# A gated recurrence's decay factors: the 64-token level and the decays to a chunk's end computed by ScalarE with a bias per row

## The chip, the cores and the metric

One core of one Trainium2 chip runs the kernel. The metric is the device time of one execution in microseconds (us). Its engines work in parallel, each through its own queue in order: PE (TensorE, the matmuls; PEld is its weight load), DVE (VectorE), ACT (ScalarE), POOL (GpSimd), and SP (SyncE), which here only issues DMAs.

## The reference, cut to what matters

The whole is one decoder layer with three parallel token mixers (a gated linear recurrence "A", a gated recurrence "B" with a convolution, and sparse attention "C"), for a prompt of 1024 tokens and 8 samples of one token each. Only mixer A on the prompt matters here, four heads of 128 keys by 128 values:

```python
    log_f = jnp.logaddexp(jnp.log(lb), jnp.log1p(-lb) + jax.nn.log_sigmoid(af.astype(jnp.float32)))
    ka = -jnp.expm1(log_f)
    ...
    def step(S, xs):
        qi, ki, vi, gi = xs
        b = jnp.cumsum(gi, axis=2)
        inter = jnp.einsum('bhtk,bhkv->bhtv', qi * jnp.exp(b), S)
        diff = b[:, :, :, None, :] - b[:, :, None, :, :]
        decay = jnp.exp(jnp.where(causal, diff, -jnp.inf))
        att = jnp.sum(qi[:, :, :, None, :] * ki[:, :, None, :, :] * decay, axis=-1)
        intra = jnp.einsum('bhts,bhsv->bhtv', att, vi)
        b_last = b[:, :, -1:, :]
        S_new = jnp.exp(b_last[:, :, 0, :])[..., None] * S + jnp.einsum('bhsk,bhsv->bhkv', ki * jnp.exp(b_last - b), vi)
```

## The kernel before, in words

PE makes all projections as three matmuls for each product (a high and a low part of both operands), and this fills most of the time. In the part about mixer A the projections of head h (the items P0 to P11; for the last pass G0 to G11, the merge gates' projections) are interleaved by hand with the recurrence of head h-1. Every engine walks the same written list, `a_items(h)` (lines 578 to 595), for five passes h = 0 to 4. The items that matter:

- P0 to P11: projections. P3 to P5 give the forget gate. At P5 ScalarE makes two passes over the whole row (Exp, then Ln, lines 1894 and 1895), then VectorE four (lines 2397, 2398, the scan 2400 and 2401), which give `b`, the running sum of the log decay, and `bk`, which is `b` minus the key's logarithm. The event `a_scan` follows.
- F (once per head) and R0, R2, R4 (one each): a *batch* of factors for 256 tokens (two chunks of 128), four batches for each head, 16 in all. GpSimd makes differences of `b` and `bk` into a ring `DD` of 6 slots (`differences`), ScalarE takes Exp of each into the tile `XQ` (`a_exps`), VectorE multiplies the query half of each by `q` (`a_factors`, lines 2417 and 2411).
- R0 to R7: one chunk of 128 tokens each. PE multiplies the factors of all levels (`a_levels`, line 1492 for the levels 64, 32 and 16), VectorE masks and adds them (lines 2427, 2428, 2431), PE turns the decayed keys (line 1504, copied back by ScalarE at line 1944) and, one chunk later, multiplies with the values and the state (`a_output`, lines 1517 to 1520). PE may start the levels of a chunk only when VectorE has masked the chunk before (`att_masked`, fired by line 2428) and when the batch is done (`x_ready`).
- Q, then N two items later in the next pass: ScalarE squares a head's output (line 1949); PE sums it with ones (lines 1535 and 1538), ScalarE takes Ln and Exp (lines 1960 and 1962).
- S: the samples' states on GpSimd (line 969 and on). GpSimd also splits each weight half into its high and low part (lines 907 and 908) at fixed items.

The chunk of 128 tokens is divided in levels 64, 32, ... 1: in each block of 2m tokens the keys of the first half get exp(b[middle] - bk), the queries of the second exp(b - b[middle]). With the two that are left, the decay of the keys to the chunk's end and exp(b - bk) for the diagonal, a batch has 9 differences. Items of the batch for level m are two GpSimd operations (lines 953 and 954), the other two one each (961 to the chunk's end, 956 for the diagonal). Each operation waits for its own end before the next is issued (`Steps`, line 151). `d_exp` counts a batch's Exps, nine for each.

The order around the third batch of a head (q = 2) is, on PE: P4, R2 (levels of chunk 2, output of chunk 1), P5, R3, P6, (in odd passes P7,) R4. In ScalarE's queue the batch stands in R2, ahead of P5's work; in VectorE's queue the products stand ahead of P5's four passes, and those ahead of R3's mask.

Of the kernel before, what the change touches and what calls it, by code (L numbers as in the profile page):

```python
# [22 lines left out]
ACT = mybir.ActivationFunctionType  # L23
AX = mybir.AxisListType.X
MUL, ADD, SUB, MAX, MIN = ALU.mult, ALU.add, ALU.subtract, ALU.max, ALU.min

P = 128
D = 1024
KT = D // P
NS = 8  # L30
# [241 lines left out]
def layer_program(nc, ctx, a, o):  # L272

    def sb(name, off, shape, dt=F32, parts=P):
        n = 1
        for x in shape:
            n *= x
        size = n * (2 if dt == BF16 else 4)
        assert 4 * off + size <= 4 * END, (name, off, size)
        t = nc.alloc_sbuf_tensor_at(name, [parts] + list(shape), dt, offset=BASE + 4 * off)  # L280
        return t[tuple([slice(None)] * (len(shape) + 1))]
# [163 lines left out]
    XQ = sb("xq", o_, [2, 10, XR]); o_ += 2 * 10 * XR  # L445
    DD = sb("dd", o_, [ND, XR]); o_ += ND * XR
    EL = sb("el", o_, [2, 2]); o_ += 8
    SGA = sb("sga", o_, [TC]); o_ += TC
    MSK = sb("msk", o_, [6, P]); o_ += 768
    STA = sb("sta", o_, [P]); o_ += 128  # L450
# [71 lines left out]
    def e(name):  # L522

        if name not in ev:
            ev[name] = sem(name)
        return ev[name]  # L540
# [336 lines left out]
    def _(pool):  # L877
# [59 lines left out]
        def differences(h, q):  # L937

            S = AS[h % 2]
            c0 = NS + XR * q  # L940
            pool.wait_ge(e("a_scan"), h + 1)
            for i in range(9):
                kk = (4 * h + q) * 9 + i
                if kk >= ND:
                    pool.wait_ge(e("d_exp"), kk - ND + 1)
                dd = DD[:, kk % ND]
                if i < 7:
                    m = LEVELS[i]
                    bv = S["b"][:, c0:c0 + XR].rearrange("p (n two m) -> p n two m", two=2, m=m)
                    dv = dd.rearrange("p (n two m) -> p n two m", two=2, m=m)  # L950
                    ref = bv[:, :, 0, m - 1:m].to_broadcast([P, XR // (2 * m), m])
                    kv_ = S["bk"][:, c0:c0 + XR].rearrange("p (n two m) -> p n two m", two=2, m=m)
                    st(nc.gpsimd.tensor_tensor(dv[:, :, 0, :], ref, kv_[:, :, 0, :], SUB))
                    st.fire(nc.gpsimd.tensor_tensor(dv[:, :, 1, :], bv[:, :, 1, :], ref, SUB), e("d_ready"))
                elif i == 8:
                    st.fire(nc.gpsimd.tensor_tensor(dd, S["b"][:, c0:c0 + XR], S["bk"][:, c0:c0 + XR], SUB), e("d_ready"))
                else:
                    bv = S["b"][:, c0:c0 + XR].rearrange("p (n m) -> p n m", m=P)
                    ref = bv[:, :, P - 1:P].to_broadcast([P, XR // P, P])
                    kv_ = S["bk"][:, c0:c0 + XR].rearrange("p (n m) -> p n m", m=P)  # L960
                    st.fire(nc.gpsimd.tensor_tensor(dd.rearrange("p (n m) -> p n m", m=P), ref, kv_, SUB), e("d_ready"))

        def sample_states(h):

# [689 lines left out]
    def _(act):  # L1654
# [267 lines left out]
        def a_exps(h, q):  # L1922
            S = AS[h % 2]
            c0 = NS + XR * q
            qq = 4 * h + q
            act.wait_ge(e("a_scan"), h + 1)
            if qq >= 2:
                act.wait_ge(e("chunk_full"), 2 * (qq - 1))
            for i in range(9):
                kk = qq * 9 + i  # L1930
                act.wait_ge(e("d_ready"), kk + 1)
                st(A(XQ[:, qq % 2, i if i < 7 else i + 1, :], DD[:, kk % ND], ACT.Exp), e("d_exp"))
            if qq >= 2:
                act.wait_ge(e("s_ready"), 2 * (qq - 1))

            st(A(XQ[:, qq % 2, 7, :], S["b"][:, c0:c0 + XR], ACT.Exp))
            bl = S["b"][:, c0:c0 + XR].rearrange("p (n m) -> p n m", m=P)[:, :, P - 1:P]
            st(A(EL[:, qq % 2, :].rearrange("p (n o) -> p n o", o=1), bl, ACT.Exp), e("eb_ready"))

# [115 lines left out]
    def _(v):  # L2055
# [327 lines left out]
        def a_group(h, i):  # L2383
            S = AS[h % 2]
            c = i % 3
            cc = slice(CH * c, CH * c + CH)
            if i < 3 or (i >= 6 and h % 2):
                n = a_product(h, i)
                v.wait_ge(e("sg_ready"), n + 1)
                if i < 3:  # L2390
                    dst = S["q"][:, cc]
                else:
                    dst = AS[(h - 1 if i < 9 else h) % 2]["z"][:, cc]
                st(stt(dst, in0=SGA[:, cc], scalar=1.0, in1=ps[:, 1 - n % 2, 0:CH], op0=ADD, op1=MUL), pq.free)
            if i == 5:
                v.wait_ge(e("sp_ready"), h + 1)
                st(stt(S["bk"], in0=S["b"], scalar=0.0, in1=SGA, op0=MAX, op1=ADD))
                st(stt(S["b"], in0=S["b"], scalar=0.0, in1=SGA, op0=MIN, op1=SUB), e("a_lf"))

                st(V.tensor_tensor_scan(S["b"][:, NS:TC], RM, S["b"][:, NS:TC], 0.0, MUL, ADD))  # L2400
                st(tt(S["bk"][:, NS:TC], S["bk"][:, NS:TC], S["b"][:, NS:TC], ADD), e("a_scan"))

        def a_factors(h, q):
# [240 lines left out]
```

## Time and profile before

| | us |
|---|---|
| median of 3 runs | 1803.81 |
| lowest and highest | 1794.69, 1806.71 |
| the profiled execution | 1793.93 |
| its span, first to last instruction | 1792.1 |

In the profile a row of the timeline is: start, duration, engine, line, operation, what it writes and reads by the program's names, shapes, how many instructions; in brackets the idle time of the engine ahead of it and what ended it. Times of day are us from the span's start. The recurrence lies at 1045 to 1360.

### The profile page before, as it was taken

The page shows a single profiled execution, that of the slowest core. Times are in us where ns is not written, and L with a number is a line of the kernel's source. Part 1 is how long each engine was busy: PE and PEld are TensorE (multiplying, and loading weights), DVE is VectorE, ACT ScalarE, POOL GpSimd, SP SyncE. Part 2 cuts the span into 40 slices and gives each one's busy share as a digit, 9 for nine tenths or more (in the row PEclk, how much of TensorE's full clock was granted, in tenths as well). Part 3 has the DMA queues.
Part 4 walks back from the last instruction along what each step waited for, and adds up shares of the span by engine and source line. Part 5 has one row for each costly group of instructions (what it writes and reads, how often), then busy time and mean ns, then how long its engine had stood idle before and what let it go on. Part 6 is the DMA issues. An engine that isn't in the chain of part 4 may idle for free. (4 is left out here: it accounts for less than half of the span.)

```text
span 1792.1 us, 30521 instructions
## 1 busy us (share of the span) xinstructions
PE 1612.0 (90%) x11996; PEld 1418.2 (79%) x11996; DVE 901.9 (50%) x1431; ACT 562.7 (31%) x1111; POOL 473.8 (26%) x461
## 2 busy tenths in 40 slices
PE   7899988988896799999989998989899986999997
PEld 3788975666665688888869998888799976899997
DVE  1651366666661222332223358857873373557577
ACT  0312135545451323222211233626352466000100
POOL 2012101000002112111131357657663122135500
PEclk9899999999998899999999999989999998999999
DMA  9321120000004444434223301202032110544422
GB/s 303 125 60 49 25 84 1 1 1 1 1 2 109 111 113 123 115 107 126 75 93 121 119 25 36 68 29 73 25 97 74 26 50 25 171 143 149 167 84 83
DMA packets 162433, 142.89 MB, mean 80 GB/s; under 512 B 50902, under 2 KB 152306, under 8 KB 161522
## 3 DMA queue, kind: packets, MB, share of 16 engines
q1 hardware_dynamic: 153298, 127.20, 23.5%
q10 hardware_dynamic: 8992, 13.74, 2.2%
q8 instruction: 95, 1.56, 0.4%
q14 instruction: 48, 0.39, 0.1%
HBM read 115.62 MB, written 29.40 MB: 81 GB/s over the span
## 5 line engine op out<-in xcount | busy, mean ns | idle before, releaser
L1016 PE MATMUL ps<-w_hi,h_hi 128*128 128x256 f32 x792 | 228.5, 289 | 5.9 <-DVEq L151 2.9
L1016 PE MATMUL ps<-w_lo,h_hi 128*128 128x256 f32 x792 | 223.7, 282 | 0.0
L1016 PE MATMUL ps<-w_hi,h_lo 128*128 128x256 f32 x792 | 223.6, 282 | 0.0
L1016 PE MATMUL ps<-h_hi,w_hi 128*128 128x344 f32 x600 | 199.1, 332 | 3.1 <-ACT ak L1960 1.4
L1016 PE MATMUL ps<-h_lo,w_hi 128*128 128x344 f32 x600 | 193.2, 322 | 0.0
L1016 PE MATMUL ps<-h_hi,w_lo 128*128 128x344 f32 x600 | 192.7, 321 | 0.0
L1016 PE MATMUL ps<-h_hi,wg_hi 128*128 128x344 f32 x432 | 146.3, 339 | 14.2 <-ACT gate_stage L1806 13.3
L1016 PEld LDWEIGHTS ps<-w_hi,h_hi 128*128 128x128 f32 x792 | 150.9, 191 | 8.0 <-DVEq L151 3.3
L1016 PEld LDWEIGHTS ps<-w_hi,h_lo 128*128 128x128 f32 x792 | 150.8, 190 | 0.0
L1016 PEld LDWEIGHTS ps<-w_lo,h_hi 128*128 128x128 f32 x792 | 150.8, 190 | 0.0
L907 POOL CAST w_hi<-w_raw 128x1024 fp32r<-128x1024 f32 (+1 forms) x48 | 52.5, 1094 | 356.2 <-DMA w_raw<-in_w_in 165.9
L1016 PE MATMUL ps<-h_lo,wg_hi 128*128 128x344 f32 x432 | 140.5, 325 | 0.0
L1016 PE MATMUL ps<-h_hi,wg_lo 128*128 128x344 f32 x432 | 140.2, 324 | 0.0
L1016 PEld LDWEIGHTS ps<-h_hi,w_hi 128*128 128x128 f32 x600 | 114.7, 191 | 6.3 <-issue 3.9
L1016 PEld LDWEIGHTS ps<-h_lo,w_hi 128*128 128x128 f32 x600 | 114.3, 191 | 0.7 <-issue 0.2
L1016 PEld LDWEIGHTS ps<-h_hi,w_lo 128*128 128x128 f32 x600 | 114.2, 190 | 0.0
L908 POOL TENSOR_TENSOR w_lo<-w_raw,w_hi 128x1024 fp32r<-128x1024 f32 (+1 forms) x48 | 112.9, 2352 | 3.8
L918 POOL TENSOR_TENSOR qt<-qt,to 128x512 f32<-128x512 f32 x16 | 20.3, 1267 | 331.6 <-DVE to L2242 331.6
L1016 PEld LDWEIGHTS ps<-h_hi,wg_hi 128*128 128x128 f32 x432 | 83.6, 193 | 29.8 <-issue 14.5
L1755 ACT ACTIVATE pr<-ps,nm 128x640 f32<-128x640 f32 (+7 forms) x128 | 88.6, 698 | 54.0 <-DVE nm L2203 42.5
L1225 PE MATMUL ps<-const_g,pr 128*128 128x128 f32 x560 | 82.0, 279 | 21.0 <-ACT pr L1755 8.2
L1806 ACT ACTIVATE gate_stage<-ps 128x344 f32<-128x344 f32 x54 | 24.7, 458 | 214.9 <-PE ps L1016 212.5
(446 smaller groups left out, 3623.4 us busy)
## 6 DMA issues: line engine op xcount, KB each, us to landing
w_raw<-in_w_in SPq DMA_DIRECT2D x46, 512.0 KB, 4.9
sgm<-gate_spill SPq DMA_DIRECT2D x22, 516.0 KB, 6.2
gate_spill<-gate_stage ACTq DMA_DIRECT2D x54, 172.0 KB, 2.4
w_raw<-in_w_in SPq DMA_DIRECT2D x34, 256.0 KB, 4.4
adw<-in_ada_w SPq DMA_DIRECT2D x8, 1024.0 KB, 11.3
pgc<-in_cache_nsa_kv SPq DMA_DIRECT2D x128, 64.0 KB, 2.4
pg<-in_cache_nsa_kv SPq DMA_DIRECT2D x64, 128.0 KB
w_raw<-in_w_branch SPq DMA_DIRECT2D x12, 512.0 KB, 5.2
```

The source lines that it names most:

```text
L907: st(nc.gpsimd.tensor_copy(hi[:, k, 0:width], raw))
L908: st.fire(nc.gpsimd.tensor_tensor(lo[:, k, 0:width], raw, hi[:, k, 0:width].bitcast(F32), SUB), half_split)
L918: st(nc.gpsimd.tensor_tensor(d3, d3, TO[:, i % 2, :].rearrange("p (a c) -> p a c", a=4), ADD), e("to_added"))
L1016: last = mm(out, lhsT=l, rhs=r, start=(first and i == 0 and j == 0), stop=(final and i == n - 1 and j == 2), skip_group_check=joint)
L1225: last = nc.tensor.transpose(ps[:, 4 + way, P * i:P * i + P], PR[:, u % 2, P * j:P * j + P], ID)
L1755: st.fire(A(PR[:, u % 2, P * n * g:P * n * g + P * n], src, ACT.Exp, bias=NM[:, 4 * (u % 2) + g:4 * (u % 2) + g + 1], scale=-1.0, accum_ou ...
L1806: st(A(GST[:, s], ps[:, 1, 0:CH], ACT.Tanh, scale=0.5), gate_free)
```

## The change

The 64-token level and the decays to the chunk's end no longer go through GpSimd. ScalarE's activation computes func(scale * in + bias) with a bias for each partition (each of the 128 keys), and within one chunk these references are one column. For the level 64 that makes four activations of 64 columns (two for each chunk of the batch), for the chunk's end two of 128. The negative of `b` in the chunk's middle, which the query half needs as bias, is made by one VectorE operation per head (128x8) between the scan and the pass of line 2401. GpSimd makes 7 differences a batch in place of 9; the diagonal's is now the seventh. ScalarE does the level 64 first, then the seven from the ring (levels 32 to 1, diagonal), then the two of the chunk's end; the events still count nine for each batch.

```diff
+    NMID = sb("nmid", o_, [2, NT]); o_ += 16
...
             pool.wait_ge(e("a_scan"), h + 1)
-            for i in range(9):
-                kk = (4 * h + q) * 9 + i
+            for kk, i in enumerate((1, 2, 3, 4, 5, 6, 8), 7 * (4 * h + q)):
                 if kk >= ND:
-                    pool.wait_ge(e("d_exp"), kk - ND + 1)
+                    pool.wait_ge(e("d_exp"), 9 * ((kk - ND) // 7) + (kk - ND) % 7 + 2)
                 dd = DD[:, kk % ND]
...
-                elif i == 8:
+                else:
                     st.fire(nc.gpsimd.tensor_tensor(dd, S["b"][:, c0:c0 + XR], S["bk"][:, c0:c0 + XR], SUB), e("d_ready"))
-                else:
-                    bv = S["b"][:, c0:c0 + XR].rearrange("p (n m) -> p n m", m=P)
-                    ref = bv[:, :, P - 1:P].to_broadcast([P, XR // P, P])
-                    kv_ = S["bk"][:, c0:c0 + XR].rearrange("p (n m) -> p n m", m=P)
-                    st.fire(nc.gpsimd.tensor_tensor(dd.rearrange("p (n m) -> p n m", m=P), ref, kv_, SUB), e("d_ready"))
...
-            for i in range(9):
-                kk = qq * 9 + i
+            half = XR // 2
+            for x in range(2):
+                k0 = c0 + half * x
+                st(A(XQ[:, qq % 2, 0, half * x:half * x + 64], S["bk"][:, k0:k0 + 64], ACT.Exp, bias=S["b"][:, k0 + 63:k0 + 64], scale=-1.0))
+                st(A(XQ[:, qq % 2, 0, half * x + 64:half * x + half], S["b"][:, k0 + 64:k0 + half], ACT.Exp, bias=NMID[:, h % 2, 2 * q + x:2 * q + x + 1]),
+                   e("d_exp") if x else None)
+            for kk, i in enumerate((1, 2, 3, 4, 5, 6, 9), 7 * qq):
                 act.wait_ge(e("d_ready"), kk + 1)
-                st(A(XQ[:, qq % 2, i if i < 7 else i + 1, :], DD[:, kk % ND], ACT.Exp), e("d_exp"))
+                st(A(XQ[:, qq % 2, i, :], DD[:, kk % ND], ACT.Exp), e("d_exp"))
+            for x in range(2):
+                k0 = c0 + half * x
+                st(A(XQ[:, qq % 2, 8, half * x:half * x + half], S["bk"][:, k0:k0 + half], ACT.Exp, bias=S["b"][:, k0 + half - 1:k0 + half], scale=-1.0),
+                   e("d_exp") if x else None)
...
                 st(V.tensor_tensor_scan(S["b"][:, NS:TC], RM, S["b"][:, NS:TC], 0.0, MUL, ADD))
+                mid = S["b"][:, NS:TC].rearrange("p (n m) -> p n m", m=P)[:, :, 63:64]
+                st(ts(NMID[:, h % 2, :].rearrange("p (n o) -> p n o", o=1), mid, -1.0, None, MUL))
                 st(tt(S["bk"][:, NS:TC], S["bk"][:, NS:TC], S["b"][:, NS:TC], ADD), e("a_scan"))
```

## Rows read from the trace of the kernel before

**Rows 1.** The page's first part: busy us, share of the span, instructions of each engine.

```profile
PE 1612.0 (90%) x11996; PEld 1418.2 (79%) x11996; DVE 901.9 (50%) x1431; ACT 562.7 (31%) x1111; POOL 473.8 (26%) x461
```

**Rows 2.** Windows view of the recurrence: length, busy us of each engine, PE clock, DMA.

```profile
1045.00:1360.00 315.00, 286.77 (x2265) 272.99 (x2265) 235.96 (x332) 142.19 (x308) 210.15 (x292) 0.96 0.18 54
```

**Rows 3.** Waits of PE, 1045 to 1360: us in total, times, longest.

```profile
PE ps L1492 <- DVE msk L2428: 17.2, 5, 7.7
PE ps L1535 <- ACT ak L1949: 4.7, 3, 1.8
PE ps L1492 <- DVEq L151: 2.0, 1, 2.0
PE ps L1016 <- ACT ak L1960: 1.4, 1, 1.4
```

**Rows 4.** Instructions on the tile dd: times of one in ns (min/median/max), first and last start.

```profile
L1932 ACT ACTIVATE xq<-dd x144: 416/418/422, 1047.3 to 1335.4; 128x256 f32<-128x256 f32 x144
L953 POOL TENSOR_TENSOR dd<-ab,ak x112: 401/460/1434, 1032.1 to 1332.3; 128x128 f32<-128x128 f32 x112
...
L961 POOL TENSOR_TENSOR dd<-ab,ak x16: 616/618/667, 1048.7 to 1333.2; 128x256 f32<-128x256 f32 x16
```

**Rows 5.** Single lines in the same form: short, biased and unbiased ones, a small copy.

```profile
L1938 ACT ACTIVATE el<-ab x16: 204/205/206, 1051.8 to 1336.3; 128x2 f32<-128x2 f32 x16
...
L1885 ACT ACTIVATE sga<-ps x24: 457/458/460, 1000.8 to 1290.4; 128x344 f32<-128x344 f32 x24
...
L2019 ACT ACTIVATE br<-ps,prm x12: 547/547/549, 1407.0 to 1503.4; 128x344 f32<-128x344 f32 x12
...
L2446 DVE COPY ot<-ps x4: 166/167/168, 1118.3 to 1349.9; 128x8 f32<-128x8 f32 x4
```

**Rows 6.** Timeline of ACT from head 0's third batch to the end of P5.

```profile
1075.06 4.02 ACT L1932 ACTIVATE xq<-dd 128x256 f32<-128x256 f32 x9 [0.48 <-PE ps L1520]
...
1083.15 1.07 ACT L1895 ACTIVATE sga<-sga 128x1032 f32<-128x1032 f32 x1
```

**Rows 7.** Timeline of DVE, then of PE, behind it.

```profile
1084.26 1.47 DVE L2397 SCALAR_TENSOR_TENSOR ak<-ab,sga 128x1032 f32<-128x1032 f32 x1 [0.74 <-ACT sga L1895]
...
1091.58 0.42 DVE L2428 TENSOR_TENSOR msk<-ps,lm 128x256 f32<-128x256 f32 x1
...
1092.15 0.53 PE L1492 MATMUL ps<-xq 128*64 128x64 f32 x14 [3.01 <-DVE msk L2428]
```

**Rows 8.** Timeline of ACT, then PE, at a head's first batch and the norm.

```profile
1125.16 4.02 ACT L1932 ACTIVATE xq<-dd 128x256 f32<-128x256 f32 x9
...
1129.89 1.06 ACT L1949 ACTIVATE ak<-ot 128x1032 f32<-128x1032 f32 x1
...
1131.01 0.84 PE L1535 MATMUL ps<-ak,ones 128*128 128x344 f32 x2 [1.46 <-ACT ak L1949]
```

**Rows 9.** Timeline of DVE at the very first batch.

```profile
1047.78 6.43 DVE L2417 TENSOR_TENSOR xq<-xq,aq 128x128 f32<-128x128 f32 x7 [15.74 <-ACT xq L1932]
```

**Rows 10.** Timeline of DVE, then of POOL, at head 0's fourth batch.

```profile
1098.88 6.96 DVE L2417 TENSOR_TENSOR xq<-xq,aq 128x128 f32<-128x128 f32 x7
...
1100.45 2.36 POOL L908 TENSOR_TENSOR w_lo<-w_raw,w_hi 128x1024 fp32r<-128x1024 f32 x1
...
1103.09 1.94 POOL L969 TENSOR_TENSOR sts<-sts,ln 128x1024 f32<-128x1024 f32 x1
```

**Rows 11.** Timeline of DVE, then of PE, at chunk 1's mask and chunk 2's levels.

```profile
1069.04 0.42 DVE L2428 TENSOR_TENSOR msk<-ps,lm 128x256 f32<-128x256 f32 x1
...
1072.24 0.55 PE L1492 MATMUL ps<-xq 128*64 128x64 f32 x14
```

**Rows 12.** Windows view, columns as in rows 2: behind three waits of PE.

```profile
1055.36:1058.77 3.41, 3.41 (x27) 3.35 (x26) 1.12 (x3) 0.26 (x1) 3.14 (x8) 0.50 0.44 133
1092.91:1096.32 3.41, 3.41 (x18) 3.41 (x17) 3.20 (x7) 0.28 (x1) 0.00 (x0) 0.50 0.00 0
...
1131.00:1134.40 3.40, 3.39 (x16) 2.80 (x17) 3.05 (x7) 2.29 (x4) 3.16 (x8) 1.00 0.00 0
```

## The prediction

> **What bounds the kernel now.** I read the page's first part, then the windows of the recurrence, then PE's waits in it, then the timelines of ScalarE, VectorE, GpSimd and PE around each wait. The first part [rows 1] shows PE busy for 90% of the span: the kernel is bound by PE, and another engine's work counts only where PE waits for it. In the recurrence [rows 2] PE is busy for 287 of 315 us, so 28 us are PE's idle time, and the waits [rows 3] say whose they are: 17.2 us in five places before the first matmul of a chunk's levels, released by VectorE's mask of the chunk before; 4.7 us in three places before the norm's matmuls, released by ScalarE's square; 2.0 us once for the first batch of factors; 1.4 us once behind the norm's logarithm. GpSimd, busy for 210 of the 315 us, releases none of PE's long waits. So the question is which of these chains gets longer or shorter.
>
> **ScalarE's price of a batch.** Before, nine Exps of 256 columns start 0.45 us apart (4.02 us from the first start to the last end, one taking 0.418 [rows 4, 6]: (4.02 - 0.418) / 8 = 0.45, so a gap of 0.032). The change removes two of them, 0.90 us. It adds four of 64 columns and two of 128, all with a bias from memory. No row has such an instruction, so I work it out. Without a bias: 2 columns take 0.205 and 256 take 0.418 [rows 4, 5], 0.84 ns a column, so 64 columns take 0.257 and 128 take 0.311. The bias: 344 columns from PSUM take 0.458 without and 0.547 with one [rows 5], 0.09 more. So 0.257 + 0.09 + 0.032 = 0.379 four times is 1.52, and 0.311 + 0.09 + 0.032 = 0.433 twice is 0.87; together 2.39 - 0.90 = **1.49 us more per batch**. The lower bound takes no surcharge for the bias: 4 x 0.289 + 2 x 0.343 - 0.90 = 0.94. The upper takes for each of the six what the 344-column biased one takes: 6 x 0.579 - 0.90 = 2.57. I take 1.49, since columns and bias are both taken from rows close by. 16 batches make 24 us of ScalarE's time, of which only that on a chain to PE counts. No table load is added: all these are Exps.
>
> The Trainium skill (ScalarE: Activation LUTs, What ACT_TABLE_LOAD costs) gives 280 ns + 0.833 ns a column for an activation with a bias from memory, but says that back-to-back ones overlap by some 93 ns. By that overlap the added part would be cheaper by 6 x 0.09, about 1.0 us a batch; here the gaps show no overlap, because each instruction waits for its own end.
>
> **GpSimd's side.** Per batch it loses two operations for the level 64 and one for the chunk's end, 0.46 + 0.41 + 0.62, with gaps 1.6 us, 26 us in all [rows 4]. It pre-makes six of the ring's slots in either kernel. Before, with the first Exp done it still has to make three items, and is through 2.8 us after the batch's start. After, its first freed slot is level 32's, 1.52 + 0.42 = 1.95 us after the start, and one operation of some 0.75 us is left: through at 2.7. So the weight splits behind it start where they did, and this side is worth nothing on the path; the cover is that GpSimd was waiting for ScalarE anyway. ScalarE doesn't wait for GpSimd in either.
>
> **P5, three places.** Head 0's third batch starts on ScalarE at 1075.06, and ScalarE then works without a break through the batch, P5's copies and the two long passes until 1084.22 [rows 6]. VectorE, done with its products, waits 0.74 us for exactly that, then makes its four passes and R3's mask until 1092.0, and PE, waiting for 3.01 us, starts chunk 4's levels at 1092.15 [rows 7]. The batch's start is set by PE's own output, so it doesn't move ahead. This repeats in the next two heads (VectorE's waits 0.75 and 0.74, PE's 7.72 and 3.03; the 7.72 is an even pass, with one projection fewer to cover). ScalarE's 1.49 goes fully into each. VectorE adds the new 128x8 operation in the same chain: 0.167 for a copy of that size [rows 5] and a gap, 0.20; nothing is its lower bound and 0.45 (a 128x256 one of line 2428, 0.42 [rows 7]) the upper; I take 0.20. 3 x 1.69 = **5.1 us**. Queued behind in ScalarE: chunk 3's key copy and P6's Tanh, which PE doesn't need before that wait ends.
>
> **The norm, three places.** A head's first batch (F) stands ahead of the square Q in ScalarE's queue. It starts at 1125.16, right behind P11's activation, the square starts at 1129.89 without a gap, and PE waits for it 1.46 us [rows 8]; likewise 1.80 and 1.45 us in the next two passes. 3 x 1.49 = **4.5 us**. The later 1.4 us for line 1960 hangs on the same chain and only moves along.
>
> **The first batch, once.** VectorE has waited 15.7 us for the first Exp [rows 9]. Its first product now comes at 1.52 in place of 0.45 us. The products then run beside GpSimd's split, one of them for the split's whole length, and only the number that is left behind it changes, from one to two or so. Bounds 0 and 1.1; I take **0.5**. The wait of 2.0 us grows by it.
>
> **The fourth batch, in two places.** PE waits 1.79 and 1.68 us for R5's mask, which stands behind the products. There ScalarE is ahead: the products start at 1098.88 since VectorE was busy; the new first Exp would be ready at 1096.54 + 1.52. They take 6.96 us, since a product beside a GpSimd operation lasts as long as that does (one beside line 908's 2.36, one beside line 969's 1.94 [rows 10]). Line 969 waits for a ScalarE result (line 1973) behind the batch, which comes 1.49 later; three or four more products then get through ahead of it. Bounds: nothing, and all of the 1.6 us; I take 0.8 each, **-1.6 us**.
>
> The Trainium skill (GPSIMD Engine Reference, the specifications) says that GpSimd's memory interfaces are shared with VectorE and contended by its two-input operations. The trace agrees, as the last paragraph shows; by that rule alone the change would help, and this is a rival below.
>
> In the other batches the 1.5 us is covered by PE's own projections: with head 0's second, for one, the mask of chunk 1 is through at 1069.46 and PE comes to chunk 2's levels at 1072.24, without a wait [rows 11]. The nearest of them leaves 1.7 us (head 1's second). If that cover were gone each would cost up to 1.5.
>
> **PE's clock.** Behind the waits of 2.0 and 3.0 us stands a stretch of 3.4 us at the granted clock 0.50, the 1.2 GHz level; behind the norm's 1.46 none [rows 12], nor behind the other two of the norm. PE-bound work loses half of such a stretch, 1.7 us. The norm's waits become 2.9 to 3.3 us, like those that have one. None to all three: 0 to 5.1; I take two, **3.4 us**. For P5's the low stretch exists already, and I change nothing.
>
> The Trainium skill (TensorE: Matmul & The Clock Gate, What's actually happening) says that the gate follows how busy the array has been and halves the rate of an idle one. By it, all three could pay; that is part of the third rival.
>
> **Sum.** 5.1 + 4.5 + 0.5 - 1.6 + 3.4 = +11.9 us, on 1793.93 us (span 1792.1 and 1.8 around it): 1805.8 for a run like the profiled one. That run is 9.9 below the median, 1803.81. The four known times (1793.93, 1794.69, 1803.81, 1806.71) have the mean 1799.8; the forecast is 1799.8 + 11.9, about **1812 us**.
>
> **Rivals.**
> - *GpSimd's relief decides (faster).* Place: VectorE's products. If VectorE and not ScalarE set the ends, the lost GpSimd operations would take away both waits of the fourth batch (3.5) and a low stretch (1.7), and 0.4 at each P5 chain: -6.4, 1793 us. It decides if the products of the third batch end later than ScalarE's P5 work, that is if VectorE's 0.74 us wait for ScalarE is replaced by no wait. Against it: that wait is there, in three heads, and grows. Chance 0.06.
> - *The gain and loss are covered (no change).* The batch's addition is near its lower bound, the clock stays, and the fourth batch gives all: 3 x 1.14 + 3 x 0.94 + 0 - 3.2 = +3, 1803 us. Also here if a later stage took the delay back; against that, mixer B starts from a chain behind the recurrence's last output. Chance 0.12.
> - *The clock pays too (slower by over 1%).* All three norms get a low stretch (5.1), two P5 waits, then 4.7 us, a second one (3.4), the fourth batch gives nothing: 5.1 + 4.5 + 0.5 + 5.1 + 3.4 = +18.6, 1818 us. Against: behind the 3.01 us wait stood one stretch only, and more waiting ahead of it needn't add one. The upper bound of the activations (1.08 more in six places, 6.5) leads to about the same, +18.4. Chance 0.19.
> - *The forecast*, +5 to +17: 0.63.
>
> **Range and chances.** From 1799.8: the covered case without its lowest part gives 1800, and the slower one on a run of the upper level (1806.7 + 18.6) gives 1825. I take 1800 to 1826. One per cent, 18 us, is about what a measurement of this kernel can tell from no change. Slower by over that: the slower rival, 0.20. Faster by over that would need three times the first rival, or a price that I have with the wrong sign: 0.04. Within: 0.76.
>
> **What would show it.** The four short Exps at 0.35 us and the two at 0.40; a batch of 13 activations at 5.5 us; VectorE's wait at P5 of 2.2 in place of 0.74; PE's waits before chunk 4's levels 4.7, 9.4 and 4.7, before the norm about 2.9, 3.3 and 2.9; GpSimd's busy time down by some 24 us. It would be wrong if the short biased Exps take 0.26 or 0.5, if PE's wait for line 1949 doesn't grow, if new waits stand before R2 or R6, or if half-clock stretches come or go in other places than these.

## The result and the profile after

| | before | after |
|---|---|---|
| median, us | 1803.07 (12 runs) | 1806.07 (12 runs) |
| lowest and highest | 1790.37, 1810.27 | 1803.44, 1815.88 |
| the profiled execution | 1793.93 | 1805.53 |
| its span | 1792.1 | 1803.7 |

The ratio is 1.0041, interval 1.0022 to 1.0059: the change makes the kernel slower by some 7 us (4.0 to 10.6), less than one per cent. The two profiled executions differ by 11.6 us, more than the means (6.9) or the medians (3.0) do.

The first part of the page after stands against [rows 1]: busy us of each engine.

```profile
PE 1620.9 (90%) x11996; PEld 1422.7 (79%) x11996; DVE 898.3 (50%) x1435; ACT 584.2 (32%) x1175; POOL 453.1 (25%) x413
```

ScalarE has 21.5 us more, GpSimd 20.7 less. PE executes the same 11,996 matmuls and is busy for 8.9 us longer: its clock was lower, 0.961 over the span where it had been 0.968. The windows view of the recurrence answers to [rows 2], PE's waits there to [rows 3] (us in total, times, longest):

```profile
1045.00:1360.00 315.00, 280.49 (x2193) 265.14 (x2191) 227.69 (x326) 162.06 (x369) 184.73 (x242) 0.93 0.17 50
```

```profile
PE ps L1487 <- DVE msk L2434: 19.3, 3, 9.6
PE ps L1530 <- ACT ak L1953: 9.1, 3, 3.3
PE ps L1487 <- DVEq L151: 2.8, 1, 2.8
...
PE ps L1011 <- ACT ak L1964: 0.8, 1, 0.8
```

PE starts 72 matmuls fewer in this window, and the mean clock in it fell from 0.96 to 0.93. Before, the mask released five waits of 17.2 us; now three of 19.3: the two of the fourth batch are gone and the three of P5 have grown. The norm's three went from 4.7 to 9.1 us. The four rows together: 25.3 us before, 32.0 after.

The prices of the new instructions, as times of one in ns (min/median/max), first and last start:

```profile
L1932 ACT ACTIVATE xq<-dd x112: 416/418/423, 1050.4 to 1346.6; 128x256 f32<-128x256 f32 x112
L1927 ACT ACTIVATE xq<-ak,ab x32: 347/348/351, 1048.8 to 1343.1; 128x64 f32<-128x64 f32 x32
...
L1935 ACT ACTIVATE xq<-ak,ab x32: 401/402/404, 1053.5 to 1347.5; 128x128 f32<-128x128 f32 x32
```

The prediction had 0.347 and 0.401. Head 0's P5 chain, to be laid beside [rows 6, 7], on VectorE and then PE:

```profile
1088.00 1.52 DVE L2401 SCALAR_TENSOR_TENSOR ak<-ab,sga 128x1032 f32<-128x1032 f32 x1 [2.19 <-ACT sga L1890]
...
1093.43 0.30 DVE L2406 TENSOR_SCALAR nmid<-ab 128x8 f32<-128x8 f32 x1
...
1096.32 0.75 PE L1487 MATMUL ps<-xq 128*64 128x64 f32 x14 [4.86 <-DVE msk L2434]
```

VectorE waits 2.19 us for ScalarE's last pass in place of 0.74, and PE 4.86 us in place of 3.01. The fourth batch of the same head, beside [rows 10], on VectorE and then GpSimd:

```profile
1103.05 5.51 DVE L2423 TENSOR_TENSOR xq<-xq,aq 128x128 f32<-128x128 f32 x7
...
1108.60 0.42 DVE L2417 TENSOR_TENSOR xq<-xq,aq 128x256 f32<-128x256 f32 x1
...
1105.08 2.35 POOL L909 TENSOR_TENSOR w_lo<-w_raw,w_hi 128x1024 fp32r<-128x1024 f32 x1
...
1108.81 1.97 POOL L964 TENSOR_TENSOR sts<-sts,ln 128x1024 f32<-128x1024 f32 x1
```

The last product is issued at 1108.60, GpSimd's 1.97 us operation only at 1108.81: no product starts beside it any more, by 0.2 us. Both waits that PE had behind such batches, 1.79 and 1.68 us, are gone whole.

The clock, in the windows view behind the first P5 wait, the first norm wait, and the third norm wait (columns as in rows 2):

```profile
1094.97:1101.80 6.83, 5.48 (x35) 5.36 (x36) 6.37 (x11) 0.93 (x3) 0.28 (x1) 0.50 0.00 0
1134.00:1137.40 3.40, 3.28 (x16) 2.69 (x17) 3.12 (x5) 2.29 (x4) 3.17 (x6) 1.00 0.01 2
1303.19:1313.43 10.24, 8.57 (x23) 6.60 (x24) 6.75 (x6) 6.51 (x8) 9.69 (x14) 0.50 0.01 2
```

Before, the P5 wait had a stretch of 3.41 us at 0.50, the 1.2 GHz level [rows 12]; now it has 6.83. Behind the first norm wait (2.93 us) the clock stays at 1.00; at the second (3.28 us) it is at 0.50 for 3.41 us, and at the third (2.92 us) for 10.24 us. Counted over the same matmuls in both profiles, from the first batch to just behind the last norm (1050 to 1387 before, 1052 to 1399 after), PE is busy at half clock for 36.8 us, before for 26.4.

So the profiled 11.6 us are: 1.5 from ahead of the recurrence, where nothing is changed (the first batch's Exps start at 1048.8 in place of 1047.3); in the recurrence 6.7 in the waits and 4.4 that PE is busy for longer with the same matmuls (half of the 10.4 us more at half clock would be 5.2), less 0.4 in its short gaps; and behind it 0.6 less. The profiled execution of the kernel before was also one with little half clock: 115.5 us in all, where the mean of 69 executions on the other occasions is 135. That is a reason why this pair differs by more than the means do.

### The profile page after: what moved, and what is told of

The parts are those of the page before. It is cut to its first block and busy times, and to the rows that moved or that the text cites. A ratio compares the mean times of both kernels' runs of the same rounds, so it can differ in the third digit from the quotient of the medians.

```text
span 1803.7 us, 30511 instructions
## 1 busy us (share of the span) xinstructions
PE 1620.9 (90%) x11996; PEld 1422.7 (79%) x11996; DVE 898.3 (50%) x1435; ACT 584.2 (32%) x1175; POOL 453.1 (25%) x413
## 5 line engine op out<-in xcount | busy, mean ns | idle before, releaser
L919 POOL TENSOR_TENSOR qt<-qt,to 128x512 f32<-128x512 f32 x16 | 20.3, 1268 | 333.8 <-DVE to L2246 333.8
```

Source lines behind the costliest of these rows:

```text
L919: st(nc.gpsimd.tensor_tensor(d3, d3, TO[:, i % 2, :].rearrange("p (a c) -> p a c", a=4), ADD), e("to_added"))
```

## The experiments

The theory going in: ScalarE's added time lengthens the chains at P5 and at the norm, GpSimd's relief does nothing by itself. The rivals: GpSimd's side decides; the clock decides; another engine covers it. In what follows "waits" are all waits of PE over 0.6 us of the one profiled execution, from the first batch to just behind the last norm, over the same matmuls in every kernel (27.2 us before, 33.9 after; the rows above leave out the last two, 1.14 and 0.74 us, which both kernels have behind 1360), and "half clock" is the mean over all runs of an execution's time at the 1.2 GHz level, from its span and mean granted clock: (1 - clock) x 2 x span. Each ratio is to the kernel before on the same chip.

**ScalarE's load alone.** The kernel before, with four unneeded 64-column Exps at the head of each batch, written to a tile of their own:

```diff
+            for x in range(4):
+                st(A(JUNK, S["b"][:, c0:c0 + 64], ACT.Exp, bias=S["b"][:, c0:c0 + 1]))
             for i in range(9):
```

> The kernel before, with four extra Exps of 64 columns with a bias at the head of each of the 16 batches, into a scratch tile that nobody reads; GpSimd's work is the old one. That is 1.52 us more of ScalarE per batch, as much as the change adds (1.49), and nothing of what it takes from GpSimd. Theory (ScalarE's longer batch makes the loss): PE's waits before chunk 4's levels go from 3.0, 7.7 and 3.0 us to 4.5, 9.3 and 4.5, those before the norm from 1.46, 1.80 and 1.45 to 2.9, 3.3 and 2.9; the span gets 6 to 12 us longer. It says of the fourth batch's waits (1.79 and 1.68 before, gone in the changed kernel): they are gone here too, since what removed them is that line 969 waits longer for ScalarE. Rival (GpSimd's lighter work removed them, and the loss at P5 is partly the new VectorE operation): the fourth batch's waits stay at 1.7 or grow to over 3.

Measured: 1.0084 (1.0053 to 1.0114; 5 runs), median 1817.46, a mean of 13.9 us more than before, where 6 to 12 were expected. PE's waits, then ScalarE, VectorE and GpSimd at head 0's fourth batch:

```profile
PE ps L1493 <- DVE msk L2431: 23.0, 5, 9.2
PE ps L1536 <- ACT ak L1952: 9.3, 3, 3.3
```

```profile
1101.29 1.50 ACT L1931 ACTIVATE junk<-ab 128x64 f32<-128x64 f32 x4 [0.69 <-PE ps L1521]
...
1109.70 2.00 DVE L2414 TENSOR_TENSOR xq<-xq,aq 128x256 f32<-128x256 f32 x1
...
1109.48 1.95 POOL L970 TENSOR_TENSOR sts<-sts,ln 128x1024 f32<-128x1024 f32 x1
```

The norm's 9.3 is that of after, and P5's waits (4.47, 9.16, 4.47) are those of after less 0.4 for the VectorE operation that is missing here. So ScalarE's load alone lengthens the six waits as the change does and costs at least as much as the whole change: this is the cause of the loss. But the theory also had the fourth batch's waits gone here, and they grew to 2.43 each: GpSimd's 1.95 us operation starts 0.2 us ahead of the last product, and the product lasts 2.00 us in place of 0.42. With nine differences to make, GpSimd begins the weight split 4.33 us after the batch's start; before it was 2.73, after 2.77. So the removed differences are worth something: they take back what ScalarE's late start costs GpSimd.

**GpSimd's relief alone.** The kernel before, where ScalarE's two Exps for the level 64 and the chunk's end read `b` itself (256 columns, no bias, so those factors hold other numbers) and GpSimd makes seven differences:

```diff
-            for i in range(9):
+            for kk, i in enumerate((1, 2, 3, 4, 5, 6, 8), 7 * (4 * h + q)):
...
+            st(A(XQ[:, qq % 2, 0, :], S["b"][:, c0:c0 + XR], ACT.Exp), e("d_exp"))
+            for kk, i in enumerate((1, 2, 3, 4, 5, 6, 9), 7 * qq):
...
+            st(A(XQ[:, qq % 2, 8, :], S["b"][:, c0:c0 + XR], ACT.Exp), e("d_exp"))
```

> The kernel before, in which GpSimd makes only seven differences per batch, as in the change, and ScalarE still makes nine Exps of 256 columns without a bias; the Exps of the level 64 and of the decay to the chunk's end read b in place of the differences, so these two factors are left out of what is computed (the output is another one, the work of ScalarE, VectorE and PE is the same in size). Theory (GpSimd's relief is worth nothing on the path): waits before chunk 4's levels 3.0, 7.7, 3.0 and before the norm 1.5, 1.8, 1.5 stay as before within 0.3, and the time is that of before within 4 us. Rival (GpSimd's relief is worth much, and the change would have been faster without its bias): at least 3 us of PE's waits in the recurrence go.

Its control, with the same two sources but GpSimd's nine differences left in place:

```diff
-                st(A(XQ[:, qq % 2, i if i < 7 else i + 1, :], DD[:, kk % ND], ACT.Exp), e("d_exp"))
+                st(A(XQ[:, qq % 2, i if i < 7 else i + 1, :], S["b"][:, c0:c0 + XR] if i in (0, 7) else DD[:, kk % ND], ACT.Exp), e("d_exp"))
```

> The kernel before, in which the Exps of the level 64 and of the decay to the chunk's end read b in place of the differences (these two factors are left out of what is computed) while GpSimd still makes all nine differences. It is the control for the kernel whose GpSimd made seven, which took 0.9928 of the time of before although its waits had shrunk by only 3 us. Theory (that gain is GpSimd's lighter work): this one takes 1.00 of the time of before within 0.3%, with waits of 3.0, 7.7, 3.0, 1.8 and 1.7 us. Rival (it comes from the other data in the matmuls or from the moment of the measurement): it takes 0.993 to 0.996.

Measured: 0.9928 (0.9901 to 0.9955; only 4 runs) and 0.9981 (0.9953 to 1.0009). The first is 12.1 us faster than before, where the theory allowed 4, and its waits fell by 2.5 us, where the rival wanted 3: neither was met whole. PE's waits for the mask, of the first and of the control:

```profile
PE ps L1491 <- DVE msk L2428: 15.0, 5, 7.5
```

```profile
PE ps L1492 <- DVE msk L2428: 18.4, 5, 7.7
```

The data do nothing that can be measured; the relief is worth about half a per cent: 0.9928 / 0.9981 = 0.9947, with the two intervals combined 0.991 to 0.999. Against the control, VectorE's 128 products take 83.2 us in place of 91.4, the fourth batch's waits are 1.37 and 0.63 in place of 1.43 and 3.21, and P5's 2.75 in place of 3.02. (The control does the same work as the kernel before and still has 3.21 where that has 1.68: single waits at the fourth batch vary from profile to profile.) The half clock is 119.9 us where the control has 133.8, which by the half is another 7 us. That the clock's part comes from these waits is the likely reading and not shown; the two kernels also ran on different occasions.

**The two parts of the change apart.** Only the level 64 (the chunk's end as before), then only the chunk's end (the level 64 as before). The diff is ScalarE's part of the first, against the kernel after; GpSimd makes eight differences in both:

```diff
-            for kk, i in enumerate((1, 2, 3, 4, 5, 6, 9), 7 * qq):
+            for kk, i in enumerate((1, 2, 3, 4, 5, 6, 8, 9), 8 * qq):
...
-            for x in range(2):
-                k0 = c0 + half * x
-                st(A(XQ[:, qq % 2, 8, half * x:half * x + half], S["bk"][:, k0:k0 + half], ACT.Exp, bias=S["b"][:, k0 + half - 1:k0 + half], scale=-1.0),
-                   e("d_exp") if x else None)
```

> The changed kernel with its chunk-end part undone: GpSimd makes that difference again and ScalarE its one Exp of 256 columns. By the measured times of one (0.347, 0.418, 0.032 between) a batch has 4 x 0.379 - 0.450 = 1.07 us more of ScalarE than before, in place of 1.49. Theory (each PE wait in that chain is the batch's length): waits before chunk 4's levels near 4.4, 9.1 and 4.4 us (4.86, 9.56, 4.86 in the changed kernel), before the norm 2.5, 2.85 and 2.5 (2.93, 3.28, 2.92). Rival (the waits come in steps of what GpSimd and VectorE do beside each other): they differ from these by over 0.5 us.

> The kernel before with the chunk-end part of the change alone: two biased Exps of 128 columns a batch behind the eight of the ring, GpSimd one operation of 0.62 us less. ScalarE 2 x 0.434 - 0.450 = 0.42 us more a batch, and the first Exp comes as early as before. Theory: waits before chunk 4's levels 3.4, 8.1 and 3.4 us, before the norm 1.9, 2.2 and 1.9; the fourth batch's waits of 1.79 and 1.68 get shorter by up to the 0.65 us that GpSimd saves; +1 to +2.5 us in sum, within what can be told from no change. Rival (GpSimd's relief outweighs it): PE's waits in the recurrence in sum are less than before.

Measured: 1.0030 (1.0007 to 1.0052) and 0.9996 (0.9969 to 1.0023). PE's waits, level 64 alone and then the chunk's end alone:

```profile
PE ps L1492 <- DVE msk L2435: 21.7, 5, 9.3
PE ps L1535 <- ACT ak L1954: 7.9, 3, 2.9
```

```profile
PE ps L1491 <- DVE msk L2431: 16.9, 5, 7.9
PE ps L1534 <- ACT ak L1952: 5.9, 3, 2.2
```

P5 measured 4.56, 9.28, 4.56 against an expected 4.4, 9.1, 4.4, and the norm 2.52, 2.86, 2.52 against 2.5, 2.85, 2.5. For the chunk's end alone 3.19, 7.91, 3.19 against 3.4, 8.1, 3.4, and 1.87, 2.21, 1.87 against 1.9, 2.2, 1.9. At the norm each wait grows by ScalarE's added time, 1.06 for the four short Exps (1.07 more per batch than the one they replace) and 0.41 for the two of 128 columns (0.42 more). At P5 the first adds 1.55, the new VectorE operation included. The second adds only 0.18 there: VectorE's wait for ScalarE does grow by 0.42, to 1.16, but its first pass behind it lasts 1.23 us in place of the 1.47 of [rows 7]. In the time the short Exps show and the two of 128 columns, with a difference fewer for GpSimd, don't. The fourth batch's waits come and go without an order: 1.20 and 2.12 in the first, 1.90 and 0.74 in the second, none in the change.

**The square ahead of the batch.** Kernel after; ScalarE makes the square before the next head's first batch:

```diff
                 elif kind == "F":
-                    a_exps(h, 0)
+                    if h == 0:
+                        a_exps(h, 0)
...
                 elif kind == "Q":
                     a_square(h - 1)
+                    if h < 4:
+                        a_exps(h, 0)
```

> The changed kernel, in which ScalarE makes the square of a head's output ahead of the next head's first batch, not behind it. Theory (the norm's waits of 2.9, 3.3 and 2.9 us are the batch standing ahead of the square): all three waits go below 0.5 us, the first batch then starts some 2.5 us later and PE does not notice, since it reaches the first chunk later than that; 9 us less than the changed kernel by the waits and up to 5 more by the clock. Rival (the norm's waits come from VectorE's or PE's side, or the delayed batch makes a new wait before chunk 0's levels): waits of over 1 us stay in sum, and the time stays within 4 us.

Measured: 1.0018 (1.0000 to 1.0035). PE's waits:

```profile
PE ps L1533 <- ACT aq L1913: 3.8, 1, 3.8
PE ps L1499 <- ACT ak L1966: 3.4, 2, 1.7
PE ps L1487 <- ACT ak L1964: 2.9, 2, 1.4
```

The theory fails here and the rival holds: the waits go at the norm's matmuls, and the batch then delays what stands behind it. Over the six places that is 11.0 us in place of the 9.9 of lines 1530 and 1011, and a wait of 1.87 us at a fourth batch is back. Swapping these two steps in ScalarE's queue only moved the cost along.

**The first batch further ahead.** Kernel after, and then the kernel before: ScalarE makes a head's first batch inside the projections, behind P9's or P10's activation, where PE has projections of its own to do:

```diff
                 if kind == "P":
                     a_group(h, i)
+                    if h and i == (10 if h % 2 else 9):
+                        a_exps(h, 0)
...
-                    a_exps(h, 0)
+                    if h == 0:
+                        a_exps(h, 0)
```

> The changed kernel, in which ScalarE makes a head's first batch one or two items earlier, behind P10's activation in the passes with 12 projections to the features and behind P9's in the other, where it sits idle, so that the square is alone behind P11. The products of VectorE stay where they are. Theory (the norm's waits of 2.93, 3.28 and 2.92 us are the batch ahead of the square, and only its place makes them): they go below 1 us in sum and nothing takes their place, since the batch now ends before PE's last chunk asks for ScalarE's key copy, or at most 1 us after; 8 us less than the changed kernel, and more where a half-clock stretch goes. Rival (as when the square was put first, the wait moves on to another step of ScalarE): PE's waits in the recurrence in sum stay within 2 us of the changed kernel's 34.1.

> The kernel before, with a head's first batch made earlier by ScalarE, at the place that took the changed kernel from 1.0041 to 0.995. Theory (the norm's waits are the batch ahead of the square, whatever its length): waits of 1.46, 1.80 and 1.45 us go, 4.7 in all, and the fourth batch's of 1.8 and 1.7 stay; 0.995 to 0.998. Rival (GpSimd, with two more operations for each batch, has the differences ready so late that ScalarE's key copy and PE's output wait): new waits of over 2 us, 1.00.

Measured: 0.9950 (0.9924 to 0.9975) and 0.9956 (0.9936 to 0.9976). Kernel after with the edit: ScalarE around the batch and the square, and PE's longest row of waits:

```profile
1118.08 0.35 ACT L1927 ACTIVATE xq<-ak,ab 128x64 f32<-128x64 f32 x1
...
1127.65 1.07 ACT L1953 ACTIVATE ak<-ot 128x1032 f32<-128x1032 f32 x1 [1.53 <-DVEq L151]
```

```profile
PE ps L1487 <- DVE msk L2437: 19.3, 3, 9.6
```

The same row of the kernel before with the edit:

```profile
PE ps L1492 <- DVE msk L2431: 20.8, 5, 7.7
```

The batch starts at 1118.08 and ScalarE is idle ahead of the square: the three norm waits are gone in both kernels, P5's 19.3 us stand untouched. Against 1.0041 without the edit, the kernel after gains 0.9% of its time, and the kernel before, which has 4.7 us of norm waits and not 9.1, 0.4%. For the kernel before it was expected that the fourth batch's waits stay at 1.8 and 1.7; the row shows that they did not: they are 1.52 and 5.48, the second because three products in turn ran beside GpSimd operations (1.87, 1.87 and 2.52 us). So its waits fell by 1.1 us and not by 4.7, and the gain of 7.4 us isn't explained by them. With this edit no difference between the two kernels can be measured, but that isn't the norm's chain alone: the kernel after still has 5.5 us more at P5, and the kernel before 7.0 us at the fourth batch, which the kernel after doesn't have.

**VectorE's passes behind the mask.** Kernel after, and then the kernel before: VectorE's four long passes of the next head (P5) are made after R3's mask and not ahead of it:

```diff
                 if kind == "P":
                     a_group(h, i)
+                    if i == 5 and h == 0:
+                        a_scan_passes(h)
...
                     if i:
                         a_chunk(h - 1, i - 1)
+                    if i == 3 and h < 4:
+                        a_scan_passes(h)
```

> The changed kernel, in which VectorE makes its four passes behind P5 after chunk 3's mask, sum and state, not ahead of them. PE's wait before chunk 4's levels then no longer hangs on ScalarE's two passes. Theory (the waits of 4.86, 9.56 and 4.86 us are that chain: batch, P5 on ScalarE, passes on VectorE, mask): they go below 1 us each, some 19 us in all, of which a few come back as waits behind the later passes; the span gets 12 to 22 us shorter than the changed kernel's 1803.7. Rival (something else, such as the product slots that P6 and P7 wait for, holds PE there): the waits move to a projection's first matmul and the span stays within 5 us.

> The kernel before, with VectorE's four passes behind P5 put after chunk 3's mask, sum and state. Theory: waits of 3.0, 7.7 and 3.0 us shrink as they did in the changed kernel (19.3 to 7.0 us there), to about 1.5 to 5 us in all, the waits before the fourth batch stay at about 1.7; 0.992 to 0.996. Rival (the changed kernel gained from this only because its chain was longer): at least 8 of the 13.8 us stay.

Measured: 0.9945 (0.9924 to 0.9967) and 0.9887 (0.9851 to 0.9922, median 1780.21). PE's waits in the kernel after with the edit:

```profile
PE ps L1011 <- DVE az L2398: 5.4, 2, 2.7
...
PE ps L1487 <- DVE msk L2436: 2.2, 2, 1.6
```

And VectorE in the kernel before with the edit, then its window of the recurrence (against [rows 2]):

```profile
1087.63 0.42 DVE L2430 TENSOR_TENSOR msk<-ps,lm 128x256 f32<-128x256 f32 x1
...
1090.39 1.39 DVE L2399 SCALAR_TENSOR_TENSOR ak<-ab,sga 128x1032 f32<-128x1032 f32 x1
```

```profile
1045.00:1360.00 315.00, 295.24 (x2365) 279.71 (x2364) 231.51 (x333) 148.36 (x317) 205.36 (x294) 0.99 0.18 55
```

The mask, at 1091.58 in [rows 7], comes at 1087.63, since it no longer stands behind passes that wait for ScalarE. In the kernel after the 19.3 us of waits for the mask become 2.2, and 5.4 us of new ones appear (VectorE's line 2398). By its ratio it is 17 us faster, within the 12 to 22 that were expected; the one profile, at 1796.6 us, is only 7 us shorter. In the kernel before the waits fall from 27.2 to 15.8 us, PE's busy time at half clock from 26.4 to 6.5, and the mean clock of the recurrence rises to 0.99. That gives back 20 us for 11 us of waits, more than the 0.992 to 0.996 that was expected. In both kernels no wait over 0.6 us at a fourth batch is left; that the kernel before would keep those of 1.7 us was expected and is wrong. P5's and the new ones together are some 6 us there, above the 1.5 to 5 foretold.

**Both moves together**, on the kernel before and on the kernel after:

> The kernel before with both moves (batch earlier, passes later). Theory: the two gains are of separate waits and add: 0.988 to 0.993, the lowest of the kernels with the old factors. Rival (the second move's gain is lost in the clock or in new waits): not below the better of the two alone by more than 0.001.

> The changed kernel with both moves. Its ScalarE chains no longer end at PE in the norm, and at P5 only by the 1.7 to 2.7 us that were left with the passes moved; GpSimd has 24 us less. If the change only cost time through these two chains, it should now be as fast as the kernel before with the same two moves, or faster by the fourth batch's 3.5 us: 0.985 to 0.991. If its ScalarE time costs elsewhere too, it is slower than that one by 0.002 or more.

Measured: 0.9871 (0.9836 to 0.9905), median 1775.3, and 0.9883 (0.9849 to 0.9916), median 1779.06. The window of the first, then the rows of PE's waits in the second:

```profile
1045.00:1360.00 315.00, 299.97 (x2386) 285.29 (x2385) 222.80 (x334) 149.34 (x319) 205.35 (x294) 0.98 0.19 59
```

```profile
PE ps L1011 <- DVE az L2401: 5.4, 2, 2.7
PE ps L1487 <- DVEq L151: 2.8, 1, 2.8
PE ps L1487 <- DVE msk L2439: 2.2, 2, 1.6
```

The kernel before with both moves has the lowest median found and beats both kernels without a move, by 1.3 and 1.7%; from the second move alone (0.9887) it can't be told apart, with 6 runs of each. It came out just below the range foretold for it, 0.988 to 0.993, and the kernel after within its own. With both chains taken apart the change costs nothing that can be measured, and gains nothing either: the intervals lie over each other.

**The clock's share.** 69 executions of the kernel before, spread over the three occasions, lasted 1787.3 to 1815.2 us, with 107 to 160 us at half clock; a line through them gives 0.49 us for each us at half clock (correlation 0.89). So most of its spread goes with the clock, at the price that PE-bound work would have. If waits of one profile and half of the mean half clock made up the mean times, they would add up, relative to the kernel before beside them, like this (for the kernel after the half clock of the runs beside it isn't on record, and the mean of the 69, 135.0 us, stands for it):

| kernel | waits | half clock / 2 | sum | measured, difference of means |
|---|---|---|---|---|
| after | +6.7 | +3.4 | +10.1 | +6.9 |
| before, ScalarE's load alone | +11.8 | +7.1 | +18.9 | +13.9 |
| before, relief alone | -2.5 | -8.1 | -10.7 | -12.1 |
| before, the relief's control | +1.2 | -1.7 | -0.5 | -2.7 |
| level 64 alone | +8.6 | +0.8 | +9.5 | +6.2 |
| chunk's end alone | +0.2 | +2.4 | +2.6 | +0.8 |
| after, square ahead of the batch | +9.7 | -0.1 | +9.6 | +3.1 |
| after, first batch further ahead | -1.8 | -1.9 | -3.7 | -8.5 |
| before, first batch further ahead | -1.1 | -2.2 | -3.3 | -7.4 |
| after, passes behind the mask | -4.9 | -3.5 | -8.5 | -8.1 |
| before, passes behind the mask | -11.5 | -12.4 | -23.8 | -19.7 |
| before, both moves | -16.1 | -10.7 | -26.8 | -22.8 |
| after, both moves | -14.2 | -8.3 | -22.4 | -20.3 |

The sums are off by 0.3 to 6.4 us, in both directions, so they rank the kernels roughly and no more.

## Why the prediction was right, and where it was not

The time foretold was 1812, measured 1806.07, in the range 1800 to 1826; slower by less than one per cent was the likeliest case. The range by itself tells little, since the median of the kernel before, 1803, lies in it too. What bears the mechanism out is the single waits. The view of the bound held: PE's idle time in the recurrence, three places at P5 and three at the norm, both behind ScalarE. Step by step:

- **ScalarE's price of a batch**, +1.49: right, 0.348 and 0.402 measured where 0.347 and 0.401 were worked out. Taking columns and bias from two different pairs of rows and adding them works.
- **P5**, +5.1: measured +1.85, +1.84 and +1.83, together +5.5. VectorE's wait is 2.19 us where 2.2 was forecast. The small difference is the new operation: 0.30 and a gap, for which 0.20 had been taken. The upper bound, 0.45, held.
- **The norm**, +4.5: measured +1.47, +1.48 and +1.47, together +4.4.
- **The first batch**, +0.5: measured +0.8, within its bounds. Line 1960's 1.4 us, which were said only to move along, shrank to 0.8.
- **The fourth batch**, -1.6: mis-sized. It gave -3.5, the whole of both waits. The mechanism was the one named: GpSimd, through with its split, now waits 1.09 us for ScalarE ahead of lines 962 and 964, where at this place it waited for nothing before, so more products get through ahead of line 964. The experiment with ScalarE's load alone shows that this needs the relief as well: there GpSimd comes later itself, and the waits grow. And I took a mean between nothing and all, where the outcome is a race: won by 0.2 us it gives everything, and in the experiment with ScalarE's load alone, lost by as little, it costs 0.6 to 0.8 more. The two waits that went were also longer than my upper bound of 1.6 each way, which came from one product's length beside the operation less its own.
- **The clock**, +3.4: somewhat small, and half of the places were wrong, which the prediction had named as a sign of being wrong. I had two norm waits take a half-clock stretch of 3.4 us each and P5's unchanged. Two of the three did take one, but the third of 10.24 us; P5's first and third doubled to 6.83 us; one of 3.41 us came at 1361. Two that stood before are gone, at 1202 and behind the fourth batch's first wait, at 1110, which the prediction didn't list. In the recurrence of the profile the clock makes 4.4 to 5.2 us. Over the runs the mean half clock is 141.8 us; that of the 12 runs beside them isn't on record, and the kernel before had means of 129.6, 136.2 and 137.1 us on the three other occasions. So 2 to 6 us of time are an estimate, and the share of the change in it isn't shown.
- **GpSimd's relief**, nothing: half right. Its splits start at 2.77 us after the batch's start as before, as foretold (2.7 and 2.8). But "worth nothing" compares with a state in which ScalarE is as early as before. With ScalarE's load and without the relief they start at 4.33, and the time is 1.0084 and not 1.0041 (a difference of 0.0007 to 0.0079). And the relief without the load, about half a per cent, was given no value: removing work from an engine that releases none of PE's waits shortened VectorE's products beside it. GpSimd's busy time fell by 20.7 us, where 24 to 26 were foretold.
- **The base and the sum.** Four times of before had the mean 1799.8, to which 11.9 were added; over 12 runs the mean is 1800.9. The change is worth about +7 by the means, 4.0 to 10.6, and the forecast's +11.9 lies outside that: it was too large. The runs tell a difference of 0.2% from none, not only the one per cent that I had taken. 2 us of the difference are the fourth batch; the rest lies within the uncertainty of the measurement and can't be put to a step. The waits and the clock of the profile, +6.7 and +4.4, come closer to the forecast than the mean of the runs does, and part of that is luck, since the profiled execution of the kernel before had some 20 us less at half clock than the mean of the 69.

What is left open: whether the clock's part of the relief comes from the shortened waits, where the 6 us come from that the kernel before gains with its first batch further ahead, and why some kernels with nearly the same waits differ by several us in half clock.

## What to carry to other kernels

Moving work between two engines that both have idle time is priced by the chains that PE waits for: here six places times 1.5 to 1.8 us. GpSimd's freed 21 us released PE nowhere directly and showed only through VectorE's products, above all in the two waits of the fourth batch. Before making a producer cheaper, see what stands ahead of the awaited result in the queue of the releasing engine: letting the mask go ahead of four passes that themselves wait brought three times what the change cost. And where a wait hangs on which of two engines issues first, don't price it by a mean; give both outcomes.

## What the runs showed of the hardware

**A VectorE product beside a GpSimd operation.** With two operands in SBUF it lasts as long as that operation: 2.00 us in place of 0.42 beside 1.95 us of GpSimd's, at most 2.44 us in place of 0.29 in the kernel after. The masks, which read PSUM, keep their time: 16 of them ran beside a long GpSimd operation in the kernel after, at 0.69 and 0.42 us as everywhere. The Trainium skill (SBUF — State Buffer, SBUF: two separate sides) calls the shared port pair an exclusive lock: whoever starts first has it for the whole instruction, the other blocks. The trace agrees, with the 0.2 us above deciding between 0.42 and 2.00 us.

**A bias from memory** adds 0.09 us to an activation of 344 columns (0.458 to 0.547 [rows 5]). At 64 and at 128 columns it adds the same by an estimate: 0.348 and 0.402 measured, against 0.257 and 0.311 between the unbiased rows of 2 and of 256 columns.

**The clock behind waits.** Waits of one length had different consequences: 2.93 us and no half-clock stretch, 2.92 us and one of 10.24 us, 3.28 us and one of 3.41 us; P5's 3.01 us had 3.41 us, its 4.86 us had 6.83 us. Over many executions of one kernel the time at half clock differed by up to 50 us, with no change in the program. The Trainium skill (TensorE: Matmul & The Clock Gate, What's actually happening) says of the ramp to full clock that its penalty is under one per cent of a typical kernel's span. Here the executions of the kernel before spread over 28 us, 1.5%, most of it along with the clock, and every effect that was studied is of that size: for a change of some us in PE's waits the clock has to be counted, as a mean over runs and not from one profile.
